# Taking the last and first blocks of each sublayer one token half at a time, with five weight places that are split in place

## The reference

```
h = rms_norm(x, g_pre) * (1 + scale) + shift
y = rms_norm(fn(h), g_post)
x = x + weight * gate * y
```

## Time and profile before

| | |
|---|---|
| time, median of 3 runs | 1643.13 us (1642.07 to 1644.82) |
| the profiled execution | 1650.7 us, its span 1648.9 us |
| PE busy | 1481.4 us (90%) |
| DVE busy | 1053.5 us (64%) |
| ACT busy | 692.8 us (42%) |
| POOL busy | 73.5 us (4%) |
| moved by DMA | 334.69 MB, mean 203 GB/s |
| share of PE in the chain that ended last | 36% of the span, DVE 5%, ACT 2%, issue 1% |

### The profile page before, as it was taken

One profiled execution on the slowest core, in us unless ns is written; L12 is line 12 of the kernel. 1 busy time (PEld: TensorE's weight loads), 2 busy tenths in 40 slices (PEclk: granted clock), 3 DMA queues, 4 the chain that ended last, 5 costly groups with the idle time before them and its releaser, 6 DMA issues. The chain is left out here.

```text
span 1648.9 us, 20189 instructions
## 1 busy us (share of the span) xinstructions
PE 1481.4 (90%) x7442; PEld 1238.0 (75%) x7442; DVE 1053.5 (64%) x1265; ACT 692.8 (42%) x708; POOL 73.5 (4%) x100
## 2 busy tenths in 40 slices
PE   1999988977999969999699898979999799899996
PEld 0788857865788847888489677858887599899784
DVE  6677766665777756776667578467665434553764
ACT  2343434434444434443456346344344344445622
POOL 0000000021000010000100002010000100000000
PEclk9999998988999979999899888989999799999998
DMA  8787841643888727876234222448664255245541
GB/s 321 301 320 301 325 178 77 257 176 127 321 318 300 307 103 280 315 295 231 80 122 153 77 77 103 153 160 320 246 254 178 78 182 197 105 154 178 204 179 64
DMA packets 49484, 334.69 MB, mean 203 GB/s; under 512 B 5488, under 2 KB 8352, under 8 KB 9376
## 3 DMA queue, kind: packets, MB, share of 16 engines
q1 hardware_dynamic: 49440, 334.10, 53.9%
HBM read 333.02 MB, written 1.06 MB: 203 GB/s over the span
## 5 line engine op out<-in xcount | busy, mean ns | idle before, releaser
L1239 DVE TENSOR_TENSOR wlo<-raw,whi 128x2048 fp32r<-128x2048 f32 x228 | 523.2, 2297 | 302.8 <-ACT whi L502 302.6
L820 PE MATMUL ps<-whi,xhi 128*128 128x512 f32 x1472 | 596.7, 405 | 62.2 <-DVE wlo L1239 42.9
L502 ACT ACTIVATE whi<-raw 128x2048 fp32r<-128x2048 f32 x228 | 435.6, 1912 | 419.1 <-PE ps L820 401.7
L820 PE MATMUL ps<-whi,xlo 128*128 128x512 f32 x1472 | 586.1, 398 | 0.0
L820 PE MATMUL ps<-wlo,xhi 128*128 128x512 f32 x1472 | 585.9, 398 | 0.0
L820 PEld LDWEIGHTS ps<-whi,xhi 128*128 128x128 f32 x1472 | 284.4, 193 | 138.3 <-issue 51.2
L820 PEld LDWEIGHTS ps<-whi,xlo 128*128 128x128 f32 x1472 | 283.9, 193 | 62.1
L820 PEld LDWEIGHTS ps<-wlo,xhi 128*128 128x128 f32 x1472 | 284.8, 193 | 57.6
L820 PE MATMUL ps<-xhi,whi 128*128 128x256 f32 x704 | 204.1, 290 | 8.5 <-ACT M L751 3.9
L1244 DVE SCALAR_TENSOR_TENSOR M<-M 128x1024 f32<-128x1024 f32 x166 | 197.3, 1226 | 11.8 <-DMA M<-ada_units 11.8
L820 PE MATMUL ps<-xhi,wlo 128*128 128x256 f32 x704 | 201.0, 286 | 0.0
(11 more groups left out here) (195 smaller groups left out, 866.0 us busy)
## 6 DMA issues: line engine op xcount, KB each, us to landing
raw<-units SPq DMA_DIRECT2D x228, 1024.0 KB, 4.8
M<-ada_units SPq DMA_DIRECT2D x83, 1024.0 KB, 6.0
M<-cvec SPq DMA_DIRECT2D x2, 512.0 KB, 5.2
x<-x_in SPq DMA_DIRECT2D x1, 1024.0 KB, 10.8
raw<-ada_units SPq DMA_DIRECT2D x1, 1024.0 KB, 17.9
M<-nw_mb SPq DMA_DIRECT2D x1, 1024.0 KB, 4.7
M<-bias_by_distance SPq DMA_DIRECT2D x2, 512.0 KB, 5.3
out<-M SPq DMA_DIRECT2D x2, 512.0 KB, 2.6
```

What stands on the lines that cost most here:

```text
L502: act.activation(whi[:, s, :], raw[:, s, :], ACT.Copy).then_inc(w_hi[s], 1)
L820: return pe.matmul(out, lhsT, rhs, start=start, stop=stop, skip_group_check=True)
L1239: dve.tensor_tensor(wlo[:, s, :], raw[:, s, :], whi[:, s, :].bitcast(F32), ALU.subtract)\
```

## The change

- There are five places (`NS`) of `raw` and `whi`; `wlo` is given the memory of `raw`, so that `lo` writes over the raw values. The load of unit u waits until PE has used unit u − 5. There are at most five units in hand.
- All hardware loops are written out. The units are renumbered in the new order of use, in which `down` of a block comes two blocks after its `up` units.
- `first_two` takes the first two blocks (four units) of each sublayer first with token half 0, then with half 1. The transposes of half 1 come between. In `ml`, `mb` and `hy` these are v, half of z and v, by token.
- The last three `down` units of an ffn sublayer, the four of `ml`, three of `mb` and the last ones of `hy` are taken first with half 0, then with half 1, and the units are released only then. `boundary` does the work of the border for half 0 while PE is at half 1. The post and pre norms work on 512 columns at a time.
- The gate row is written by SP to DRAM (`gate_rows`) and read back as a broadcast to 128 partitions. The product with ones, its POOL and ACT work and PE's wait for it go.
- The norm weights of `ml` and `mb` are applied as scales per partition when the turned blocks are split: 4 operations on ACT and 4 on DVE in place of one each.
- `ml` takes 16 ada units (before: 8), the four ffn sublayers 16, 16, 16, 12. SP issues them at fixed positions among its loads.
- In `mb`, half of z is made in `first_two`, so the scan holds 8 pieces of z, one for each second pair, not 16.
- The gated block `g` has two places and its split in `xhi`/`xlo` four. The end of `hy` is taken by token halves and by 512 columns.

```diff
-SLOTS = 3
+NS = 5
+def up_unit(n, i, half):
+    return FIRST[n] + (2 * i if i <= 2 else 3 * i - 2) + half
+def down_unit(n, j):
+    return FIRST[n] + (6 + 3 * j if j <= 8 else 22 + j)
+        wlo = nc.alloc_sbuf_tensor_at("wlo", [P, NS, UNIT], F32R, offset=first)
...
-                    sp.wait_ge(w_lo[s], n + CREDIT[s])
+                if u >= NS:
+                    sp.wait_ge(w_used, u - NS + 1)
+                sp.dma_start(raw[:, s, :], units[u, :, :]).then_inc(w_in[s], 16)
...
+            def gate_out(n):
+                sp.wait_ge(S["gate_ok"], n + 1)
+                sp.dma_start(bass.AP(gate_rows.tensor, n * D, [[KT, P], [1, KT]]), gpc[:, n, :]).then_inc(S["gd_in"], 16)
+            def gate_in(n):
+                sp.wait_ge(S["gd_in"], 16 * n + 16)
+                if n:
+                    sp.wait_ge(S["yg_ok"], 4 * n)
+                sp.dma_start(gp[:, :], bass.AP(gate_rows.tensor, n * D, [[0, P], [1, D]])).then_inc(S["gp_ok"], 16)
...
+                if kind == "ml":
+                    v = ADA_FIRST[n]
+                    for u in range(16):
+                        load(u0 + u)
+                        for _ in range({6: 1, 7: 2, 8: 2, 9: 2, 10: 3, 11: 1, 12: 1, 14: 3, 15: 1}.get(u, 0)):
+                            load_ada(v)
+                            v += 1
...
+            def first_two(n, turned=False, after_first=None, before_last=None):
+                u = FIRST[n]
+                if not turned:
+                    turn_x(n, 0)
+                split_ok(n, 0, 0)
+                by_token(u, 0, 0, 4)
+                split_ok(n, 0, 1)
+                by_token(u + 1, 1, 0, 4).then_inc(S["fb_ok"], 1)
+                by_token(u + 2, 0, 0, 5)
+                if not turned:
+                    turn_x(n, 1)
+                by_token(u + 3, 1, 0, 5).then_inc(S["fb_ok"], 1)
+                split_ok(n, 1, 0)
+                by_token(u, 0, 1, 6).then_inc(w_used, 1)
...
+                    last = [(down_unit(n, j), 8 + 2 * (j % 4)) for j in range(NF - 3, NF)]
+                    for j in (1, 2):
+                        pe.wait_ge(S["gt_lo"], b + NF - 2 + j)
+                        r = down(*last[j], 0, stop=(j == 2))
+                    r.then_inc(y_done[0], 1)
+                    for j in range(3):
+                        down(*last[j], 1, stop=(j == 2)).then_inc(w_used, 1)
...
+            def boundary(n, late):
+                u = FIRST[n + 1]
+                gated_y(n, 0)
+                new_x(n, 0)
+                if not late:
+                    lo(u + 1)
+                normed_x(n + 1, 0)
+                for h in range(2):
+                    turned_x(n + 1, 0, h)
+                for h in range(2):
+                    split_x(n + 1, 0, h)
+                if late:
+                    lo(u + 1)
+                gated_y(n, 1)
+                new_x(n, 1)
+                lo(u + 2)
+                normed_x(n + 1, 1)
+                lo(u + 3)
...
                     dve.tensor_scalar(G(1), G(4), -1.0, None, ALU.mult).then_inc(S["ml_rows"], 1)
+                    ada(v)
+                    lo(u0 + 7)
+                    ada(v + 1)
+                    ada(v + 2)
+                    lo(u0 + 8)
...
+                    ada(v + 12)
+                    lo(u0 + 15)
+                    ada(v + 13)
+                    lo(u0 + 16)
+                    for k in range(14, 16):
+                        ada(v + k)
+                    ada_done(v + 15)
                     mod_columns(2)
                     gate_columns(2)
+                    boundary(n, True)
...
+                        if p % 2 == 0 and p < 14:
+                            token_piece(p // 2 + 1, u0 + 16, j0 + 6)
```

More of the change, by code:

```diff
@@ L77, in on, with build @@
         return ins
[L79 to L109, removed]
+def build(nc, x_in, units, ada_units, rows, cvec, fg_row, mlw, mlb, mbw, mbv, mbd, rel, onehot, negrow, out):
     scratch = nc.dram_tensor("bias_by_distance", (H_AT, REL), F32).ap()
+    gate_rows = nc.dram_tensor("gate_rows", (7, D), F32).ap()
     ctx = ExitStack()
@@ L246, in build, with wait_used @@
         block = ctx.enter_context(nc.Block())
[L249 to L264, removed]
[L265 to L271 removed]
+        def wait_used(eng, u):
+            eng.wait_ge(w_used, u + 1)
         def wait_y(eng, n, t):
@@ L398, in _ @@
[L398 to L410 removed]
+                    load(up_unit(n, 2, 1))
@@ L489, in _ @@
+                        pre(n + 1, t)
         @block.scalar
         def _(act):
[L491 to L502 removed]
@@ new lines, in feature_piece, with down @@
+            def feature_piece(p, u, j):
+                i, part = divmod(p, 4)
+                half, b = divmod(part, 2)
+                v = u + 2 * i + half
+                if half == 0:
+                    free(b, j + i)
+                by_feature(v, half, 2 * b)
+                r = by_feature(v, half, 2 * b + 1)
+                if part == 2:
+                    r.then_inc(pj_ok, 1)
+                if b == 1:
+                    r.then_inc(w_used, 1)
+            def down(u, k, t, start=False, stop=False, bank=0, ns=(0, 1)):
+                s = u % NS
+                ready(u)
+                for kk in range(2):
+                    for n in ns:
+                        w = slice(kk * D + n * 512, kk * D + n * 512 + 512)
+                        r = three(ps[:, bank + 2 * t + n, :], xhi[:, k + kk, t * P:(t + 1) * P],
+                                  xlo[:, k + kk, t * P:(t + 1) * P], whi[:, s, w], wlo[:, s, w],
+                                  start=start and kk == 0, stop=stop and kk == 1)
+                return r
@@ L1147, in _ @@
                     turn_y(0)
-                    for t in range(T):
-                        pe.wait_ge(pj_free[t], pb + 10 + ONE)
+                    for b in range(2):
+                        free(b, j0 + 8)
                     turn_y(1)
@@ L1152, in _ @@
                     turn_y(2)
-                    for u in range(8):
+                    outs = u0 + 20
+                    for u in range(5):
                         if u == 2:
@@ new lines, in _ @@
+                    for b in range(2):
+                        free(b, j0 + 18)
+                    for u in range(4):
+                        r = down(u0 + 44 + u, 2 * u, 0, start=(u == 0), stop=(u == 3), bank=4)
+                    r.then_inc(S["hy_yc"], 1)
+                    for u in range(4):
+                        if u == 2:
+                            turn_merged(0)
+                        down(u0 + 44 + u, 2 * u, 1, start=(u == 0), stop=(u == 3), bank=4)\
+                            .then_inc(w_used, 1)
```

1638 lines of the change are left out of this document (840 added, 798 removed).

## The result

The changed kernel takes 1657.6 us (median, 1653.5 to 1660.9), the kernel before beside it 1642.6. The ratio is 1.0089, with a 95% interval of 1.0063 to 1.0115: slower by 0.9%, where 1611, and so faster, was forecast. The profiled execution took 1653.5 us, its span 1651.1.

A forecast was written before the change was run, and what follows sets the result against it. PE's borders between sublayers, not its work, were taken as the bound. Gains 13.5 − 22.5 + 1.5 + 16.6 − 16.5 + 18.1 + 21 = 31.7 gave 1619.0 profiled, less 7.6: 1611 us; range 1550 to 1648 (forecast's own 1590 to 1630).

The forecast's parts named there:

- Border of an ffn sublayer, after: Ffn sublayers: half 0's chain, 7.1 us, covered by 8.16; dense blocks 184.5 plus 10.6 overhead make 195.1 us.
- DVE's reserve of 4 us in a block: Ffn blocks: DVE's spare time per block, said to hide an in-place `lo` 0.2 us slower.
- 17 us for a unit to land: Ffn blocks, five places: 21.8 us cover landing (4.8), `hi` 1.9 and `lo` 2.3, enough unless landing passes 17.
- Rival (c): Ffn blocks: five places starve PE, 30 blocks with two ada units take 18.3 us, lose 45: 1656; chance 0.1.
- the 358 GB/s: HBM bandwidth per core from a skill page; a block's 312 GB/s fits under it, so starved blocks would not happen.
- The frame: Whole kernel: sums made against the profiled execution, 1650.7 us; 7.6 subtracted at the end for the median.
- the first stop: `ml`, before the gate columns: ninth unit's load held behind an ada load waiting for DVE; PE stalls 17 us.
- the exit: `ml`'s end: DVE's ada units, `lo` and modulation precede the border's first operation; 12.6 us idling, charged to sublayer 2.
- Rival (a): `ml` and `mb`: the stalls don't bind and the scan stays warm, 53 us faster: 1558; chance 0.2.
- (b): Scan of `mb`: PE's clock stays low throughout, 125 us rather than 101: 1635; chance 0.15.
- `hy`, +29.8 for +21: Sublayer 6: gain of 21 us, from border +10, the 5.81 wait before the last units gone, tail 2.2 shorter.
- doesn't shorten that chain, it opens gaps: Scan of `mb`: removing 8 of 16 z pieces (21.8 us of PE) leaves the chain; scan 102.6 to 101 us.

The follow-up runs named there:

- the first experiments: Follow-ups timed beside the kernel before at 1646.5 us, beginning with the changed kernel with the turned block's split put first: 1614.5 us, ratio 0.981.
- without the stagger: Last three `down` units of ffn sublayers taken unit by unit again, against the kernel with the turned block's split first: 1626.3 us, 0.989 of the kernel before.
- halves: Scan's later pieces of z cut in two, one half ahead of every pair: 1650.8 us on the changed kernel, 1553.1 us on the kernel with all corrections.
- the scan with the rows ahead: In the scan of `mb`, decay rows of pair p+2 issued ahead of y of pair p, against the changed kernel: 1628.7 us, 0.990 of the kernel before.

## Why the prediction was wrong

**The failed step** is in "Border of an ffn sublayer, after": "Sublayer: 184.5 + 10.6 = 195.1". The 184.5 is a price of dense blocks taken from the kernel before and carried over without laying out the new order of a block. For the border and the mixers all engines were laid out; for the 44 blocks, nearly half of the time, only totals were weighed: DVE's reserve of 4 us in a block, and 17 us for a unit to land. Both totals hold. But the split of the turned block, 0.7 us of work that PE needs within 10.9 us, now stood behind a `lo` whose data had just been asked for and an ada unit. In the kernel before ACT was seldom kept waiting for a landing (17.4 us in all), since a load could start when `lo` had freed its place. Now a place comes free when PE has done with it, ACT splits each unit as it lands, and its waits for landings are 298.1 us in all. In the blocks none of these cost PE a unit; they cost what was queued behind: 26 intervals of 18.2 to 18.8 where the sum had 16.8. Setting that one order right gave 43 us and brought sublayers 3 and 5 to 195.0.

**Rival (c)** has nearly the right price, 18.3 us in 30 blocks and 1656 (measured in 26), with the wrong mechanism: neither bandwidth nor landing was short (4.9 us median, against 17 needed), and the same bytes fit into 16.81. Nor are the 358 GB/s that stand behind the rivals in the prediction a ceiling here: over its first 41.3 us the changed kernel moves 382.

**The frame.** I subtracted 7.6 us, as if the changed kernel's median would lie as far below its profiled time as that of before. It lies 4.1 above. Of the miss of 46 us, 34.5 are in the profiled execution (1653.5 against 1619.0) and 11.7 here. The 13 executions of before on the chip of the first experiments span 1641.8 to 1650.7; one profiled execution has no offset that could be carried to another kernel.

**Right** were the border (3.9 us to the first product for 4.45; the chain of half 0 covered, and uncovered by 4.97 without the stagger, so it is 7.7 long and not 7.1; before the last turn 2.58 for 1.8), `ml` (161 against 160; the first stop 17 against 15.9, the exit 12.6 against 10.3), `mb` (284.6 against 285.8) and the start of the kernel (39.3 against 39.17). Gate rows by DRAM cost nothing visible. Rival (a) did not happen, (b) in part: the scan's clock is 0.68.

**A size that was off:** `hy`, +29.8 for +21. Of the 8.8, 5.5 lie in the attention, for which the sum had no term. The gap ahead of its first transposes is 2.45 us shorter (before, then after):

```profile
1406.79 0.55 PE L1180 MATMUL ps<-ident,hf 128*128 128x128 f32 x3 [3.61 <-DVE hf L1681]
```
```profile
1427.50 0.55 PE L1223 MATMUL ps<-ident,hf 128*128 128x128 f32 x3 [1.16 <-DVE hf L1789]
```

From there to the last product of the heads are 58.9 us where they were 62.0; the granted clock was 0.66 in the first 5 us of them before the change and is 1.00 after it. The last units and the tail give 4.5 more than forecast, the border about 1 less; what makes up the 4.5 was not tested.

**Two slips in the sum**, too small to matter: eleven blocks are 184.7 in its first paragraph and 184.5 in its sum, and sublayer 2 is given the gain of sublayer 3, 16.6, where its own window, 212.7, would give 17.6.

**In the scan** the cause was half right. That taking 8 of 16 pieces out "doesn't shorten that chain, it opens gaps" held. That the chain is a matter of order, decay rows behind y and exponents ahead of weights, was not seen; in the kernel before, pieces of z filled most of PE's time in every pair.

## What to carry to other kernels

When a change moves the point at which buffers come free, lay out one steady block again, engine by engine, with each operation at its place in its queue: a reserve in totals says nothing on a small operation with a near deadline that stands behind one that waits for a DMA. Put what the busiest engine needs soonest ahead of prefetched work, in every queue that it passes. A stop that is removed is worth only the distance to the next one: 13.4 us of idling gave 2.6 in `ml` while DVE was late as well, and the sublayer fell by 18.8 when DVE's ada units were moved out too.

## What the runs showed of the hardware

In the ffn borders of the changed kernel the gap of 2.90 us before the first product doesn't bring the low clock: that product takes 0.50 us, and sublayers 3 and 5 have 0.99 instead of 0.96 and 0.95. With the transposes held up by 4.97 us and a second gap of 2.48, the same product takes 0.79:

```profile
614.05 0.79 PE L815 MATMUL ps<-whi,xhi 128*128 128x512 f32 x1 [2.48 <-DVE xlo L1366]
```

The length of the last gap alone doesn't decide: in the kernel before, the first product of sublayer 5 (at 1090.97) takes 0.79 behind a gap of 2.92, with gaps of 5.33 and 1.25 ahead of that one.

In the scan the clock stays between 0.66 and 0.81 in every form that was tried, with gaps of 2.78 or with few gaps, whole pieces or halves. The section on HAM oscillation of "TensorE: Matmul & The Clock Gate" in the Trainium skill puts such falls down to idle waits between bursts. The gaps of 2.78 fit that; the scan with the rows ahead, in which PE is busy for 92% of the time and still gets 0.79, does not fit it well. What holds the clock down there, small matmuls of 64 columns or something else, was not tested and stays open.
